# Spreading the token rows of an expert over partition quads by a table, in a mixture-of-experts encoder layer

## What is computed

```python
def moe_ffn(h, w_router, b_router, w_gate, b_gate, w_up, b_up, w_down, b_down):
    ...
    logits = (t @ w_router + b_router).astype(jnp.float32)
    top_val, top_idx = lax.top_k(logits, TOP_K)          # 4 of 32 experts per token
    top_w = jax.nn.softmax(top_val, axis=-1)
    ...
    def expert_block(args):                              # rows of one expert
        xb, e = args
        g = xb @ w_gate[e] + b_gate[e]
        u = xb @ w_up[e] + b_up[e]
        g = jnp.minimum(g, SWIGLU_LIMIT)
        u = jnp.clip(u, -SWIGLU_LIMIT, SWIGLU_LIMIT)
        act = g * jax.nn.sigmoid(SWIGLU_ALPHA * g) * (u + 1.0)
        return act @ w_down[e] + b_down[e]
    ...
    out = jnp.zeros_like(t).at[row_tok].add(ys * row_w[:, None].astype(t.dtype))
```

## Time and profile before

| | |
|---|---|
| median of three runs | 1414.61 us |
| profiled execution | 1414.13 us, span 1412.2 us |
| TensorE matmul busy | 1312.2 us, 93% of the span |
| VectorE / ScalarE / GpSimd busy | 453.8 / 219.4 / 204.9 us |
| mean granted TensorE clock | 0.975 |
| bytes by DMA | 446.19 MB, of these 424.24 MB in the queue of SyncE and 17.20 MB in the queue of GpSimd |

### The profile page before, as it was taken

How to read it: one execution, slowest core, us unless ns; L and a number is a source line. 1 busy time by engine, 2 the same in 40 slices (tenths; PEclk the granted TensorE clock), 3 DMA queues, 4 the chain that set the end, 5 groups by cost and what they waited for, 6 DMA issues and landing times.

```text
span 1412.2 us, 40301 instructions
## 1 busy us (share of the span) xinstructions
PE 1312.2 (93%) x18085; PEld 800.4 (57%) x18085; DVE 453.8 (32%) x1049; ACT 219.4 (16%) x493; POOL 204.9 (15%) x150
## 2 busy tenths in 40 slices
PE   6999989998799999999998988998999998999984
PEld 3466675565456666666555555665655654666651
DVE  2674586645322222222222221322221322222210
ACT  2232243331101010110100010110110011001110
POOL 0031230000102211111221111121121121112111
PEclk9999999998899999999999999999999999999995
DMA  9100420146799999999999999999999999999993
GB/s 355 61 1 0 148 110 1 55 155 246 268 353 377 389 390 385 395 397 400 391 392 402 392 412 399 407 403 397 412 398 403 407 398 411 388 416 388 402 409 127
DMA packets 79488, 446.19 MB, mean 316 GB/s; under 512 B 13354, under 2 KB 21618, under 8 KB 30162
## 3 DMA queue, kind: packets, MB, share of 16 engines
q1 hardware_dynamic: 63504, 424.24, 74.9%
q0 software_dynamic: 15120, 17.20, 5.8%
q10 hardware_dynamic: 690, 2.13, 0.4%
HBM read 433.30 MB, written 14.94 MB: 317 GB/s over the span
## 4 chain that ended last, share of the span: by engine, by line
SPq 43%; PE 41%; DMA 8%; DVE 3%; issue 3%; ACT 1%; POOL 1%; POOLq 0%; ACTq 0%; DVEq 0%
SPq L627 43%; PE pair L1933 20%; PE pair L1669 5%; DMA ring<-in_w_down 4%; PE pair L1770 4%; PE pair L1635 4%; DMA ring<-in_w_gate 2%; PE pair L1620 1%; DVE rest L1344 1%; PE pair L1892 1%; POOL ring L747 1%; DVE ring L1091 1%; PE pair L1800 1%; DVE rest L1091 1%; SPq L601 1%
## 5 line engine op out<-in xcount | busy, mean ns | idle before, releaser
L1933 PE MATMUL pair<-ring,rest 128*32 128x256 f32 x14720 | 841.3, 383 | 44.1 <-DMA ring<-in_w_down 24.5
L1933 PEld LDWEIGHTS pair<-ring,rest 128*32 128x32 f32 x14720 | 474.8, 110 | 356.6 <-issue 31.5
L789 POOL DMA_INDIRECT out<-rest x82 | 128.2, 1564 | 773.5 <-ACT rest L1048 719.1
L1091 DVE TENSOR_TENSOR rest<-pair,rest 128x512 f32<-128x512 f32 (+4 forms) x125 | 94.5, 759 | 453.6 <-PE pair L1933 421.7
L1048 ACT ACTIVATE rest<-rest 128x256 f32<-128x256 f32 x82 | 36.5, 500 | 541.1 <-DVE rest L1091 541.1
L1030 ACT ACTIVATE rest<-rest 128x512 f32<-128x512 f32 (+3 forms) x34 | 24.4, 718 | 299.2 <-DVE rest L1446 286.3
L1669 PE MATMUL pair<-ring 128*128 128x512 f32 (+1 forms) x192 | 69.4, 521 | 0.0
L1091 DVE TENSOR_TENSOR rest<-rest 128x512 f32<-128x512 f32 (+7 forms) x84 | 58.9, 713 | 32.2 <-ACT rest L1030 26.2
L1933 PE MATMUL pair<-rest 128*32 128x256 f32 x1024 | 63.7, 389 | 4.9 <-DMA rest<-in_w_down 2.7
L1413 DVE TENSOR_SCALAR rest<-pair 64x1 int32<-64x1 f32 (+3 forms) x34 | 5.2, 152 | 179.6 <-issue 176.0
L1770 PE MATMUL pair<-ring,rest 128*128 128x512 f32 x128 | 59.4, 612 | 0.9 <-DVE rest L1091 0.9
(11 more groups left out here) (182 smaller groups left out, 871.0 us busy)
## 6 DMA issues: line engine op xcount, KB each, us to landing
ring<-in_w_gate SPq DMA_DIRECT2D x121, 1024.0 KB
ring<-in_w_down SPq DMA_DIRECT2D x121, 1024.0 KB
ring<-in_w_up SPq DMA_DIRECT2D x119, 1024.0 KB
rest<-in_w_up SPq DMA_DIRECT2D x9, 1024.0 KB
rest<-in_w_gate SPq DMA_DIRECT2D x7, 1024.0 KB
rest<-in_w_down SPq DMA_DIRECT2D x7, 1024.0 KB
ring<-in_w_in SPq DMA_DIRECT2D x8, 520.0 KB, 11.2
ring<-in_x SPq DMA_DIRECT2D x8, 512.0 KB, 8.3
```

The source lines that it names most:

```text
L789: p.indirect_dma_start(out=out_rows, out_offset=bass.IndirectOffsetOnAxis(ap=sidx[vi.ring][:, g:g + 1].bitcast(I32), axis=0), in_=yrow_b[v ...
L1091: return v.tensor_tensor(out=out, in0=a, in1=b, op=op)
L1933: last = T.matmul(ps[q * TOK:(q + 1) * TOK, g * QW:(g + 1) * QW], x, pieces[slot][:, kk, q * QW:(q + 1) * QW], start=(k == 0 and g % 2 == ...
```

## The change

**Table of places.** The columns of the one-hot matrix no longer stand for ranks 0, 1, 2, ... A table, `slot_rank`, names for each of 128 places the rank that stands there. Within a group of 32, rank r stands in quad r mod 8 (a quad is four neighbouring places), so eight consecutive ranks stand in eight quads. Of four groups, group 0 has partitions 0 to 31, group 1 has 64 to 95, group 2 has 32 to 63 and group 3 has 96 to 127 (`BLOCK_AT`).

**Width.** One-hot matrix and dispatch are 96 places wide for a visit of 1, 2 or 3 groups, 128 for 4, and 32 for a second visit (`spread`). The gather names 128 partitions in each visit but a second one. The places beyond the visit's groups get an index past the end: `far_c` adds a larger number there, and partitions 96 to 127 of the index tile are set once by two small memsets. Visits of four groups have an index tile of their own (`idx_w`). A visit of 2 groups is transposed 96 wide, and ScalarE copies out the first and the third 32 columns of each 96.

**Constants.** The full-width `iota` and the row `krow_c` give up their place in the constants to `slot_rank` and `far_c`; the key of the ranking is now made with three instructions in place of one.

```diff
+BLOCK_AT = (0, 2, 1, 3)
+
+
+def ranks_of_slots():
+
+    out = np.zeros(P, int)
+    for n in range(P):
+        g, r = divmod(n, TOK)
+        e, turn = r % 8, r // 8
+        i = 4 * e + (2 * turn + turn // 2 + e // 4) % 4
+        out[TOK * BLOCK_AT[g] + i] = n
+    assert sorted(out) == list(range(P))
+    return out
...
+    c[:, C_FAR:C_TOK] = np.where(slot_rank[:, None] < TOK * np.arange(1, MAX_GROUPS + 1)[None, :], FAR, 3 * FAR)
...
+        def spread(vi):
+            return TOK if vi.off else 3 * TOK if vi.G < MAX_GROUPS else P
+
+        def index_of(vi):
+            return idx_w[vi.b] if vi.G == MAX_GROUPS else idx_g[vi.b]
+
+        def turned_width(vi):
+            return TOK * (vi.G + (vi.G == 2))
...
+            for n in range(2):
+                nc.gpsimd.memset(idx_g[n][3 * TOK:P, :], 1.0).then_inc(s_zero, 1)
+                pool.wait_ge(s_zero, n + 1)
...
-                c = vi.G * TOK
+                c = TOK if vi.off else P
                 p.indirect_dma_start(
                     out=hrow[vi.b][0:c, :], out_offset=None, in_=hn_d,
-                    in_offset=bass.IndirectOffsetOnAxis(ap=idx_g[vi.b][0:c, :].bitcast(I32), axis=0),
+                    in_offset=bass.IndirectOffsetOnAxis(ap=index_of(vi)[0:c, :].bitcast(I32), axis=0),
...
+                    rows_, w = turned_rows(vi)[:, 4 * h * c:4 * (h + 1) * c], turned_width(vi)
+                    if w > c:
+                        rows_, src = cut(rows_, 4, 2, TOK), cut(ps[:, 0:4 * w], 4, 3, TOK)[:, :, 0:3:2, :]
...
             def onehot_tiles(vi, e, tiles):
 
-                c = vi.G * TOK
+                c = spread(vi)
...
-                    v.tensor_scalar(out=buf[:, t, :], in0=iota[:, 0:c], scalar1=vi.off + 1.0,
+                    v.tensor_scalar(out=buf[:, t, :], in0=slot_rank[:, 0:c], scalar1=vi.off + 1.0,
...
-            link(v.scalar_tensor_tensor(out=key, in0=cnt, scalar=float(NE), in1=krow_c, op0=ALU.mult, op1=ALU.add))
+            link(v.scalar_tensor_tensor(out=key, in0=cnt, scalar=float(NE), in1=iota, op0=ALU.mult, op1=ALU.subtract))
+            for e in range(FIXED):
+                ins = v.tensor_scalar(out=key[:, e:e + 1], in0=key[:, e:e + 1], scalar1=float(FIXED - e << 15), scalar2=None,
+                                      op0=ALU.add)
+            link(ins)
...
             def turn_rows(vi):
 
                 pe.wait_ge(s_gath[vi.b], 16 * (vi.gathers + 1))
-                c = vi.G * TOK
+                c = turned_width(vi)
...
-                            x = xT[:, k, g * TOK:(g + 1) * TOK] if m < 2 else aT[:, g, k % 2, k // 2, :]
+                            col = TOK * (BLOCK_AT[g] if vi.G > 2 else g)
+                            x = xT[:, k, col:col + TOK] if m < 2 else aT[:, g, k % 2, k // 2, :]
```

More of the change, by code:

```diff
@@ L146 @@
 OVER_USES = [("d", 0), ("r", 0), ("x", 0), ("x", 1), ("a", 0), ("a", 1)]
-C_LE, C_GE, C_GT, C_LT, C_ID, C_ONE, C_IOTA = (n * P for n in range(7))
+C_LE, C_GE, C_GT, C_LT, C_ID, C_ONE, C_SLOT = (n * P for n in range(7))
 C_REP = 7 * P
@@ L158 @@
 C_KCOL = C_CAP + 1
-C_KROW = C_KCOL + 1
-C_TOK = C_KROW + NE
+C_IOTA = C_KCOL + 1
+C_FAR = C_IOTA + NE
+C_TOK = C_FAR + MAX_GROUPS
 C_FOLD = C_TOK + NT
@@ L174, in constants @@
     c[:, C_ONE:C_ONE + P] = 1
-    c[:, C_IOTA:C_IOTA + P] = q
+    slot_rank = ranks_of_slots()
+    c[:, C_SLOT:C_SLOT + P] = slot_rank
+    c[:, C_IOTA:C_IOTA + NE] = q[:, 0:NE]
     half = HD // 2
@@ L195, in constants @@
     c[:, C_KCOL] = first
-    c[:, C_KROW:C_TOK] = first[None, 0:NE]
     c[:, C_TOK:C_FOLD] = np.arange(P)[:, None] + P * np.arange(NT) - FAR
@@ L280, in hybrid_layer @@
         const = take(C_END)
-        c_le, c_ge, c_gt, c_lt, ident, ones, iota = (const[:, n * P:(n + 1) * P] for n in range(7))
+        c_le, c_ge, c_gt, c_lt, ident, ones, slot_rank = (const[:, n * P:(n + 1) * P] for n in range(7))
         cos_t = cut(const[:, C_COS:C_SIN], NT, HD)
@@ L350, in hybrid_layer @@
         m8 = cut(take(NT * 8), NT, 8); ix8 = cut(take(NT * 8), NT, 8); ixf = cut(take(NT * 8), NT, 8)
-        nmx = take(NT); ws = cut(take(NT * TOPK), NT, TOPK); wsum = take(NT); wrec = take(NT)
+        nmx = qss[:, 0:NT]; ws = cut(take(NT * TOPK), NT, TOPK); wsum = qss[:, NT:2 * NT]; wrec = take(NT)
         items_f = cut(take(2 * IW), 2, IW)
@@ L354, in hybrid_layer @@
         over_n = take(1)
-        idx_g = [take(1) for _ in range(2)]
+        idx_g, idx_w = [take(1) for _ in range(2)], [take(1) for _ in range(2)]
         pay = [cut(take(NT * 2), NT, 2) for _ in range(2)]
@@ L1269, in choose @@
                 link(v.tensor_copy(ixf[:, t, :], ix8[:, t, :].bitcast(U32)))
-                link(tt(chosen[:, t, :, :], times(iota[:, 0:NE], TOPK), over(ixf[:, t, 0:TOPK], NE), ALU.is_equal))
+                link(tt(chosen[:, t, :, :], times(iota, TOPK), over(ixf[:, t, 0:TOPK], NE), ALU.is_equal))
                 v.tensor_reduce(out=msk[:, t, :], in_=chosen[:, t, :, :].rearrange("p k e -> p e k"), axis=AX.X,
@@ L1412, in index @@
                 at_least(dve, s_gath[vi.b], vi.gathers * 16)
-                v.tensor_scalar(out=idx_g[vi.b][0:c, :].bitcast(I32), in0=ps[0:c, 0:1], scalar1=FAR, scalar2=None,
+                v.tensor_scalar(out=index_of(vi)[0:c, :].bitcast(I32), in0=ps[0:c, 0:1], scalar1=far_c[0:c, vi.G - 1:vi.G], scalar2=None,
                                 op0=ALU.add).then_inc(s_idx, 1)
@@ L1491, in _ @@
             wait_taken(dve, "rnk")
-            link(v.scalar_tensor_tensor(out=itm, in0=here, scalar=1.0, in1=iota[:, 0:NE], op0=ALU.mult, op1=ALU.mult,
+            link(v.scalar_tensor_tensor(out=itm, in0=here, scalar=1.0, in1=iota, op0=ALU.mult, op1=ALU.mult,
                                         accum_out=icol[:, 1:2]))
@@ L1519, in _ @@
             link(v.scalar_tensor_tensor(out=ohi, in0=cums, scalar=row_c, in1=ohi, op0=ALU.is_le, op1=ALU.mult))
-            link(v.scalar_tensor_tensor(out=itm, in0=ohi, scalar=1.0, in1=iota[:, 0:NE], op0=ALU.mult, op1=ALU.mult,
+            link(v.scalar_tensor_tensor(out=itm, in0=ohi, scalar=1.0, in1=iota, op0=ALU.mult, op1=ALU.mult,
                                         accum_out=icol[:, 2:3]))
@@ L1586, in over_steps @@
                 for t in range(NT):
-                    v.tensor_scalar(out=buf[:, t, :], in0=iota, scalar1=items_f[:, 1, bass.ds(q, 1)],
+                    v.tensor_scalar(out=buf[:, t, :], in0=slot_rank, scalar1=items_f[:, 1, bass.ds(q, 1)],
                                     scalar2=posm[:, t, bass.ds(e, 1)], op0=ALU.add, op1=ALU.is_equal)
```

13 lines of the change are left out of this document (7 added, 6 removed).

## The result

The changed kernel takes 1393.11 us at the median of four runs (1390.39 to 1394.41), the kernel before 1414.67 us beside it. The ratio is 0.9845, with a 95% interval of 0.9825 to 0.9866: 21.5 us faster, four times the forecast and outside its range. The profiled execution took 1393.82 us with a span of 1391.4 us.

The account below looks back on a forecast made before the run. The prediction took the DMA stream of weights as the bound, its end set by the fullest engine. Terms -7.5 + 1.3 + 0.7 + 0.4 = -5.1 us gave 1409.5 us, with a range over the cases of 1403 to 1420 us.

Parts of the forecast that it names:

- Gathers: Gathered rows on engine 0 rise from 164 to 170, 1.0 us more; the gathers get no better spread.
- Naming 128 brings no engine into play, and by that rule the gathers alone would gain nothing.: Gathers of 96, 64 and 32 partitions already divide over 16 engines, so naming 128 gains nothing.
- Scatters, 7.5 us: Engine 0's added rows fall from 630 to 544, shortening the weight stream's tail; saving taken as 7.5 us, gathers included.
- Places past the end, 1.3 us: 1536 more skipped gather places, about 90 on engine 0, move no data and cost 1.3 us.
- The rival at 1418.7 us: Skipped places cost 0.117 us each, as much as an added row, making the kernel 4.1 us slower; chance 0.12.
- First gather, 0.7 us: The first gather, on the chain, gets one more row on engine 0 and lands 0.7 us later.
- TensorE, 0.4 us: Wider dispatches and transposes cost 0.4 us on the chain until 577.72 us; later ones cost nothing.
- Worth almost nothing: From 578 to 1350 us TensorE idles 42 us, so a microsecond saved on it gains almost nothing.
- VectorE, ScalarE, GpSimd: Extra key instructions, wider one-hots, strided copy and two memsets lie in idle time and cost nothing.
- The marks I gave: Signs of being right: tail under 16 us, last weight near 1395 us, 402 to 404 GB/s from 578 to 1350 us.
- my mark for a gain that is hidden: Shorter tail, same end, more SyncE waits for TensorE: the rival that slots limit the stream, 1415.2 us, chance 0.20.
- More than forecast: Rival: the scatters' full 10.1 us are saved with no cost beside them, 1404.5 us; chance 0.05.

Follow-up runs that it names:

- the base of the second set: Changed kernel with groups one after the other, two-group transposes 64 wide, gathers of 128 partitions and table kept: 1396.3 us, ratio 0.9871.
- the narrow dispatch with the table: Kernel before with all gathers naming 128 partitions and the table of places added, dispatch and transposes as narrow as before: 1391.77 us, ratio 0.9844.

## Why the prediction was wrong

The direction was right and the size was not; the range missed the time by 10 us. Its own sum went through the scatters, and the gain came through the gathers, so the right direction was in good part luck. Taken step by step:

- **Gathers.** This is the step that failed. It priced a gathered row at the weights' rate, 0.163 us before and after, and so saw only how rows are spread over engines (+1.0 us). What a narrow gather does to the packets beside it had no term. The runs put it at 17 us for each engine in the weights' queue, at 11 to 12 ns of the kernel's time for each row, and at 14 to 20 us for the one line that sets 128; with only the width changed the gain is 26 us. The 959 and 335 engine-us into which I split GpSimd's queue rested on that same price. Without rows the queue takes 0.042 x 16 x 1375.6 = 924 engine-us, so rows in narrow gathers took 1310 - 924 = 386, 0.19 us each, and in wide ones 1247 - 922 = 325, 0.16 us each, both good to 0.01: the price held for the wide ones alone.
- **"Naming 128 brings no engine into play, and by that rule the gathers alone would gain nothing."** I drew this from the Trainium skill (DMA: Bandwidth & Descriptors, Why a DMA increments its semaphore by 16 and not by 1). The rule may well hold for the number of engines; the trace does not agree that nothing is gained. The width without the table gives 0.9852, and with nothing else changed 0.9816.
- **Scatters, 7.5 us.** The table alone gives 4.8 us (2.8 to 6.9), where my whole sum was 5.1. That is agreement in size only: its tail is as long as before, and on top of wide gathers the same table gives nothing (0.9845 against 0.9852) or costs 0.28%. That the fullest engine's scatters set the end is not borne out; my count of 630 and 544 rows for engine 0 may still be right. The Trainium skill (DMA: Bandwidth & Descriptors, The descriptor swizzle) gives the assignment that I counted by for a transfer to 128 partitions; no run here names an engine.
- **Places past the end, 1.3 us.** Not dear. With every place skipped, the wide kernel has 1728 more of them than the narrow one and is 5 us faster, and GpSimd's queue takes 0.042 x 16 x 1371.6 = 922 engine-us against 924. At 0.117 us each it would have been 202 more. The rival at 1418.7 us is out. My reason was wrong all the same: a skipped place of a gather does move data, for it still reads 4 KB of memory (see the end).
- **First gather, 0.7 us.** It measured 0.44 us on the chain. The median landing rose by 1.0 us, within the two I allowed, and the gathers stayed covered but for the first.
- **TensorE, 0.4 us.** Right only as long as DMA was the bound. With 20 us of DMA time gone TensorE holds the chain 146 us longer, and more of the wider dispatches lie on it: until 723.7 us five of visits of two groups, 5 x 0.21 = 1.1 us by the earlier trace rows, and near the end the three of one group, at most 0.77 us each. The runs put it at 3.8 us (0.27% between the base of the second set and the narrow dispatch with the table), two more wide gathers included, but with overlapping intervals, so this cost is likely and not shown. "Worth almost nothing" was said of the kernel before; in the one after SyncE waits for TensorE 130.3 us.
- **VectorE, ScalarE, GpSimd.** Hidden, as forecast; none is on the chain beyond what it was.
- **The marks I gave.** The tail is 13 us in place of 16, as said. The rate was to be 402 to 404 GB/s and is 407. GpSimd's share did not rise. The last weight came at 1378.7 us, not near 1395. The rate was the mark that showed another mechanism. SyncE's waits for TensorE rose too, my mark for a gain that is hidden, but the end moved with them: what they show is the new bound.

Of the rivals none named it. "More than forecast" had the right side and the wrong cause, and its 1404.5 us were 11 us too slow.

Three things stay open. How a narrow gather's packets are dealt to engines isn't known, so why they slow their neighbours is not shown; the runs show only that it takes rows copied, that 96 and 64 cost about the same a row, and that 112 is no cure. Why the table gains 5 us with narrow gathers and nothing with wide ones is open; in the profiled executions 2.3 of the 6.1 us between their spans stand ahead of the first gather (issued at 349.28 us in place of 351.60), in the mixer, which the table doesn't touch. Open too are the 5 us between the two kernels without rows, whose weights' packets take no less time in the faster one (16,679 against 16,639); the first gather, 6.93 in place of 8.04 us, is 1.1 of them.

## What to carry to other kernels

In this kernel an indirect gather of 64, 96 or 112 partitions beside a stream that fills the DMA engines slowed that stream while the share still read as full; where yours looks like it, preset the index past the end and name all 128. To find such a thing, compare the GB/s of short windows at equal share, one for each form of the small transfer: here the kernel before had narrow and full gathers side by side, and reading eight windows would have pointed at the width before any run. And once a large DMA cost is gone, price the small steps of the next engine again: the version with the lowest median here was the one that left them as they were.

## What the runs showed of the hardware

- Gathers of 64, 96 or 112 partitions with rows, over the 12 us from 2 us after their issue: 368 to 381 GB/s on average, at a share of 1.03 to 1.04; gathers of 128 there: 402 to 404. In the 4 or 5 us windows shown the low values are 319 to 344 and the high ones 412 to 434.
- Narrow gathers that copy no row: 403 to 405 GB/s over the same 12 us.
- A skipped place of a gather still reads 4 KB of memory: the reads rose by 439.59 - 433.30 = 6.29 MB, which is 1536 places of 4 KB, and with all gathers wide by 7.08 MB, which is 1728 places of 4 KB. With every place of the narrow gathers skipped the read is 433.30 MB as before, while the queue's own count fell from 17.20 to 8.82 MB. The reads cost no time that these runs can tell.
